# Attention in two passes, with the row maxima carried through DRAM into a 97th row of the queries

## The reference

```python
scale = 1.0 / math.sqrt(QK_NOPE + QK_ROPE)          # 1 / sqrt(96)
s = einsum('bqhd,bkhd->bhqk', qn_b, k_nope) + einsum('bqhd,bkd->bhqk', qr_b, k_rope)
p = jax.nn.softmax(s.astype(jnp.float32) * scale, axis=-1)
return jnp.einsum('bhqk,bkhd->bqhd', p.astype(v.dtype), v)   # v: 64 columns per head
```

## Time and profile before

| | |
|---|---|
| median of three runs | 3265.0 us (3261.01 to 3273.98) |
| the profiled execution | 3276.46 us |
| its span | 3274.6 us |
| attention's first to last product | 527 to 1215 us |
| granted TensorE clock, mean of the span | 0.982 |

### The profile page before, as it was taken

The page is one execution under the profiler, slowest core; times in us unless marked ns, Lnnn a source line. Parts: engine busy times, 40 slices in busy tenths (PEclk is TensorE's granted clock), DMA queues, the critical chain, the costliest instruction groups (busy, mean ns, idle before and its releaser), DMA issues.

```text
span 3274.6 us, 54823 instructions
## 1 busy us (share of the span) xinstructions
PE 3152.3 (96%) x23414; PEld 2544.0 (78%) x23414; DVE 2012.7 (61%) x3047; ACT 1067.3 (33%) x1528; POOL 374.1 (11%) x354
## 2 busy tenths in 40 slices
PE   8998998899999998999999999999999999999999
PEld 7787886777777777778888888887746888788887
DVE  6665554466766775545444444469979988755544
ACT  5222334445444443222111111132253333433332
POOL 0222441000000000301000000020000000110000
PEclk9999999799999999999999999999999999999999
DMA  3343665122222223421111111111101222223222
GB/s 148 126 135 99 214 213 186 54 75 81 69 86 75 82 81 116 148 90 52 39 52 52 52 42 49 52 39 52 39 13 52 103 91 103 90 90 126 94 91 76
DMA packets 93537, 288.80 MB, mean 88 GB/s; under 512 B 12400, under 2 KB 38640, under 8 KB 72816
## 3 DMA queue, kind: packets, MB, share of 16 engines
q1 hardware_dynamic: 79104, 233.39, 21.1%
q0 software_dynamic: 14192, 51.91, 4.6%
HBM read 228.64 MB, written 56.62 MB: 87 GB/s over the span
## 4 chain that ended last, share of the span: by engine, by line
PE 82%; DVE 10%; ACT 2%; issue 2%; DMA 2%; POOL 1%; SPq 1%; DVEq 0%; ACTq 0%; POOLq 0%
PE ps L2441 24%; PE ps L307 21%; PE ps L489 7%; PE ps L1744 4%; PE ps L2247 3%; PE ps L2603 2%; PE ps L1755 2%; DVE Yh L2630 2%; PE ps L1767 2%; PE ps L2063 1%; PE ps L1387 1%; PE ps L1404 1%; PE ps L1008 1%; PE ps L1398 1%; DVE wlo L287 1%
## 5 line engine op out<-in xcount | busy, mean ns | idle before, releaser
L2441 PE MATMUL ps<-Hh,whi 128*128 128x512 f32 x1600 | 497.6, 392 | 1.3 <-DVE uA L2562 0.7
L283 ACT ACTIVATE whi<-raw 128x2048 fp32r<-128x2048 f32 x139 | 265.5, 1910 | 522.2 <-PE ps L307 296.1
L287 DVE TENSOR_TENSOR wlo<-raw,whi 128x2048 fp32r<-128x2048 f32 x139 | 321.2, 2311 | 95.0 <-ACT whi L283 94.6
L2441 PEld LDWEIGHTS ps<-Hh,whi 128*128 128x128 f32 x1600 | 300.0, 188 | 70.5 <-issue 5.3
L2441 PE MATMUL ps<-Hh,wlo 128*128 128x512 f32 x800 | 311.4, 389 | 0.0
L307 PE MATMUL ps<-Hhi,wlo 128*128 128x512 f32 x672 | 206.9, 389 | 0.0
L307 PE MATMUL ps<-Hlo,whi 128*128 128x512 f32 x672 | 206.9, 389 | 0.0
L307 PE MATMUL ps<-Hhi,whi 128*128 128x512 f32 x672 | 206.8, 389 | 0.0
L2441 PE MATMUL ps<-aHh,whi 128*128 128x512 f32 x512 | 199.5, 390 | 2.7 <-DVE wlo L287 2.5
L2441 PE MATMUL ps<-aLh,whi 128*128 128x512 f32 x512 | 199.2, 389 | 0.0
L2441 PE MATMUL ps<-aHh,wlo 128*128 128x512 f32 x512 | 199.2, 389 | 0.0
(11 more groups left out here) (389 smaller groups left out, 6181.8 us busy)
## 6 DMA issues: line engine op xcount, KB each, us to landing
raw<-in_panels SPq DMA_DIRECT2D x139, 1024.0 KB, 4.8
rwf<-F POOLq DMA_DIRECT2D x16, 1280.0 KB, 6.6
L<-rwf SPq DMA_DIRECT2D x16, 1024.0 KB, 5.0
L<-rwf SPq DMA_DIRECT2D x64, 256.0 KB, 3.5
gts<-so POOLq DMA_DIRECT2D x16, 512.0 KB, 3.5
gl<-gts SPq DMA_DIRECT2D x32, 256.0 KB, 3.6
rwt<-so POOLq DMA_DIRECT2D x15, 512.0 KB, 2.9
qkd<-XTs POOLq DMA_DIRECT2D x16, 384.0 KB, 4.0
```

What stands on the lines that cost most here:

```text
L283: e.activation(whi[i % 2][:, :], raw_of(i)[:, :], AF.Copy).then_inc(*a_hi.up(i))
L287: e.tensor_tensor(wlo[i % 2][:, :], raw_of(i)[:, :], whi[i % 2][:, :].bitcast(F32), OP.subtract).then_inc(*v_lo.up(i))
L2441: m = e.matmul(ap, W[wi][:, kc, n0:n0 + 128], mov[mi][:, kc, :], start=x == 0 and q == 0, stop=x == len(kcs) - 1 and q == 2)
```

## The change

The attention goes by eight groups g (a pair of heads k = g // 2 and a half of the queries), and each group has two passes of eight items:
- "max" j: scores of one head and 128 queries as before, but from tiles typed fp32r, into banks 4 and 5; VectorE takes the negated maxima into negm.
- the row: when a group's eight maxima are there, GpSimd's queue stores the 128x8 values to DRAM as [8, 128] (nrow) and, when that has landed, loads them into the 97th partition of the queries' tile Qr. The 97th row of the keys' tile Kr is ones, written once.
- "exp" j: the scores again, transposed: 128 keys by 512 queries for both heads, in fp32 and with 97 rows, so that the maximum is subtracted by the product. ScalarE takes the exponential straight into Pe. There are no transposes and no scaling.
- PV: two products of 512 columns, accumulated over j in bank 6 or 7. The sums over keys: GpSimd adds the Pe tiles (acc), and at a group's end TensorE multiplies acc with ones (bank 4), ScalarE copies, VectorE takes the reciprocal of 128x512, multiplies, and GpSimd stores.
The maxima pass of group g + 1 alternates with the exponent pass of group g. `slots()` stays as it was; the items are laid over its pieces.

```diff
-    Kp = [sb(f"Kp{i}", 8 * i, [96, 2, S]) for i in range(2)]
...
+    Kr = [sb(f"Kr{i}", 8 * i, [97, 2, S], F32R) for i in range(2)]
+    Pe = [sb(f"Pe{i}", 16 + 4 * i, [128, 2, 512]) for i in range(2)]
+    acc = sb("acc", 24, [128, 2, 512])
+    Qr = [sb(f"Qr{i}", (28, 170, 174)[i], [97, 2, 512], F32R) for i in range(3)]
...
+    def att_items():
+        made = [("max", 0, j) for j in range(8)]
+        for g in range(7):
+            made += [("max", g + 1, 0)]
+            for j in range(7):
+                made += [("max", g + 1, j + 1), ("exp", g, j)]
+            made += [("exp", g, 7)]
+        return made + [("exp", 7, j) for j in range(8)]
...
+            if c == "exp":
+                on.setdefault(i + (2 if g < 7 else 1), []).append(("PV", g, j))
+                on.setdefault(i + 1, []).append(("acc", g, j))
+                if j == 7:
+                    on.setdefault(i + (4 if g < 6 else 3 if g < 7 else 2), []).append(("sum", g, 0))
+                    on.setdefault(i + (5 if g < 6 else 4 if g < 7 else 3), []).append(("out", g, 0))
+            if c == "max" and j == 7:
+                on.setdefault(i + (2 if g else 1), []).append(("row", g, 0))
...
     def att_pe(e, u, c):
...
+            if name == "sum":
+                pair_free(e, "sum", g, 0)
+                e.wait_ge(*g_at.by("acc", g, 7))
+                for h in range(2):
+                    m = e.matmul(bank[4][64 * h:64 * h + 64, :], ones[:, 0:64], acc[:, h, :], start=True, stop=True)
...
+            if name == "max":
...
+                pair_free(e, "max", g, j)
+                for half in range(2):
+                    m = e.matmul(bank[4 + half], Qr[g % 3][0:96, j % 2, 128 * (j // 2):128 * (j // 2) + 128],
+                                 Kr[k % 2][0:96, j % 2, hs(half)], start=True, stop=True)
...
+                if j == 0:
+                    e.wait_ge(*d_nr.by(g, "in"))
...
+                for h in range(2):
+                    m = e.matmul(bank[4 + h], Kr[k % 2][:, h, 128 * j:128 * (j + 1)].bitcast(F32),
+                                 Qr[g % 3][:, h, :].bitcast(F32), start=True, stop=True)
...
+                e.wait_ge(*a_at.by("E", g, j))
+                for h in range(2):
+                    m = e.matmul(bank[6 + g % 2][64 * h:64 * h + 64, :], Vp[(g // 2) % 2][:, j, 64 * h:64 * h + 64],
+                                 Pe[j % 2][:, h, :], start=j == 0, stop=j == 7)
...
     def att_dve(e, u, c):
...
+        if i == 0:
+            for n in range(2):
+                e.memset(Kr[n][96:97, :, :].bitcast(F32), 1.0).then_inc(*v_at.up("ones", n))
...
+                e.reciprocal(Oh[:, :], Oh[:, :]).then_inc(*v_at.up("rec", g))
...
+                e.tensor_tensor(Oh[:, :], bank[6 + g % 2], Oh[:, :], OP.mult).then_inc(*v_at.up("O", g))
...
     def att_pool(e, u, c):
...
+            if name == "row":
+                e.wait_ge(*v_at.by("max", g, 7))
+                e.dma_start(nrow[g].rearrange("n q -> q n"), negm[:, 8 * g:8 * g + 8], allow_slow_non_contiguous=True).then_inc(*d_nr.up(g, "out"))
+                e.wait_ge(*d_nr.by(g, "out"))
+                if g >= 3:
+                    e.wait_ge(*t_at.by("B", g - 3, 7))
+                e.dma_start(Qr[g % 3][96:97, :, :].bitcast(F32), nrow[g].rearrange("(h n) q -> h (n q)", h=2)[None, :, :]).then_inc(*d_nr.up(g, "in"))
+            if name == "acc" and j:
...
+                e.tensor_tensor(acc[:, :, :], Pe[0][:, :, :] if j == 1 else acc[:, :, :], Pe[j % 2][:, :, :],
+                                OP.add).then_inc(*g_at.up("acc", g, j))
...
-        for k in range(2):
+        for k in range(3):
             q_sp(e, k)
```

More of the change, by code:

```diff
@@ L1713, in build @@
[L1713 to L1716, removed]
-    oas = dram("oas", [4, 128, S])
-    t_at, v_at, a_at = signals("t_at"), signals("v_at"), signals("a_at")
-    d_kp, d_vp, d_qb, d_oa = landings("d_kp", 2), landings("d_vp", 2), landings("d_qb", 3), landings("d_oa", 2)
+    negm = sb("negm", 40, [128, 64])
+    Oh = sb("Oh", 201.28125, [128, 512])
@@ new lines, in build @@
+    oas = dram("oas", [4, 128, S])
+    nrow = dram("nrow", [8, 8, 128])
+    d_nr = landings("d_nr", 2)
+    t_at, v_at, a_at, g_at = signals("t_at"), signals("v_at"), signals("a_at"), signals("g_at")
+    d_kp, d_vp, d_qr, d_oa = landings("d_kp", 2), landings("d_vp", 2), landings("d_qr", 3), landings("d_oa", 1)
+    def att_items():
[6 more added lines that the diff above has]
+        return made + [("exp", 7, j) for j in range(8)]
@@ new lines, in build, with also @@
+    ITEMS = att_items()
+    def also():
+        on = {}
+        for i, (c, g, j) in enumerate(ITEMS):
+            if c == "exp":
[6 more added lines that the diff above has]
+                on.setdefault(i + (2 if g else 1), []).append(("row", g, 0))
+        return on
@@ L1721, in kv_sp, with before_of @@
+    ALSO = also()
+    def before_of():
+        made, last = {}, None
+        for i in range(len(ITEMS) + 4):
+            for key in [key for key in ALSO.get(i, ()) if key[0] == "sum"] + ITEMS[i:i + 1]:
+                made[key], last = last, key
+        return made
+    PAIR = before_of()
     def kv_sp(e, k):
         if k >= 2:
-            e.wait_ge(*t_at.by("S", 16 * k - 17))
-            e.wait_ge(*t_at.by("O", 8 * k - 9))
-        e.dma_start(Kp[k % 2][:, :, :], qkd[1, :, 2 * k:2 * k + 2, :]).then_inc(*d_kp.up(k))
+            e.wait_ge(*t_at.by("B", 2 * k - 3, 7))
+            e.wait_ge(*t_at.by("PV", 2 * k - 3, 7))
+        e.dma_start(Kr[k % 2][0:96, :, :].bitcast(F32), qkd[1, :, 2 * k:2 * k + 2, :]).then_inc(*d_kp.up(k))
@@ L1726, in kv_sp @@
         e.dma_start(Vp[k % 2][:, :, :], vds[:, :, 128 * k:128 * (k + 1)]).then_inc(*d_vp.up(k))
     def q_sp(e, g):
-        k, j = g // 8, g % 8
+        k, qh = g // 2, g % 2
         if g >= 3:
-            e.wait_ge(*t_at.by("S", 2 * g - 5))
-        e.dma_start(Qb[g % 3][:, :, :], qkd[0, :, 2 * k:2 * k + 2, 128 * j:128 * (j + 1)]).then_inc(*d_qb.up(g))
-    def att_pe(e, u, c):
[L1735 to L1768, removed]
@@ new lines, in att_act @@
+    def att_act(e, u, c):
+        i = 2 * u + c
+        for name, g, j in ALSO.get(i, ()):
+            if name == "sum":
+                e.wait_ge(*t_at.by("sum", g))
+                if g:
+                    e.wait_ge(*d_oa.by(g - 1))
+                e.activation(Oh[:, :], bank[4], AF.Copy).then_inc(*a_at.up("sum", g))
+        if i < len(ITEMS):
+            name, g, j = ITEMS[i]
+            if name == "exp":
+                e.wait_ge(*t_at.by("B", g, j))
+                n = 8 * g + j - 2
+                if n >= 0:
+                    e.wait_ge(*t_at.by("PV", n // 8, n % 8))
+                    e.wait_ge(*g_at.by("acc", n // 8, max(1, n % 8)))
+                e.activation(Pe[j % 2][:, :, :], ps[:, 2048:3072].rearrange("p (h t) -> p h t", h=2),
+                             AF.Exp).then_inc(*a_at.up("E", g, j))
@@ L1822, in build @@
+    def att_sp(e, u, c):
+        i = 2 * u + c - 8
+        if i >= 0 and i % 16 == 5:
+            g = i // 16 + 2
+            if 3 <= g < 8:
+                q_sp(e, g)
+            if g in (4, 6):
+                kv_sp(e, g // 2)
     BEFORE = ("cum", "mul", "turn", "scores", "PV", "Nc")
@@ L1932, in att_over @@
         e.wait_ge(*a_at.all())
+        e.wait_ge(*g_at.all())
+        for w in d_nr.all():
+            e.wait_ge(*w)
         for w in d_oa.all():
```

96 lines of the change are left out of this document (49 added, 47 removed).

## The result

The changed kernel takes 3403.8 us (median of four, 3380.5 to 3416.8) against 3268.5 us of the kernel before, run beside it: ratio 1.041, 95% interval 1.034 to 1.047. That is 135 us slower, where 10 us of the profiled execution's time were forecast and the range ended at 3315. The forecast was wrong. The profiled execution is the one of 3380.5 us, so what follows shows about 104 of the 135 us.

The account below looks back on a forecast made before the run. TensorE, busy 96% of the span, was taken as the bound. Terms -25 - 10 + 25 + 15 + 1 + 4 = +10 us gave 3286.5 for the profiled execution, 3275 in terms of the median; range 3237 to 3315.

Parts of the forecast that it names:

- TensorE's work, -25: Attention matmuls: maxima, exponent, PV and sum products take 226 us against 251 with transposes, 25 us less.
- ScalarE, -10: TensorE's 16.1 us of waits for ScalarE's copies: the transposes' 6.9 go, part of L1358's 9.2 stays, 10 us less.
- "out", +25: Group ends: VectorE's reciprocal and multiply, 4.04 us in one piece, delay TensorE 3.3 us each; 25 us more for eight.
- GpSimd's additions, +15: 56 additions of Pe tiles hold up VectorE's instructions with two SBUF operands, 0 to 60 us; 15 us more taken.
- its worst case: Rival: VectorE and GpSimd hold each other for most of each addition, +45 us, 3310; chance 0.18.
- The row, +5 in all: Row of maxima through DRAM: trip of 9.4 us, free in six groups, 1 us more in the last, 4 in the first.
- The rival of the late row: Row's trip decides from 15 us on; at 22 us it costs 63 more, +73, 3338; chance 0.08.
- The clock: Rival: new gaps bring four more stretches of 10 us at 1.2 GHz, 5 us each, +20, 3295; chance 0.10.

Follow-up runs that it names:

- e1: Changed kernel without the row's store and load, the 97th row of Qr set once at the start: 3338.1 us, ratio 1.022.
- e4: Changed kernel without the row's trip, without reciprocals and with 8 of the 56 additions: 3309.2 us, ratio 1.013.
- h2: e4 without ScalarE's copy of bank 4, sum products kept, VectorE copying the PV bank in place of the multiply: 3278.6 us, ratio 1.003.
- f4: e4 without sum products and ScalarE's copy of bank 4, VectorE copying the PV bank in place of the multiply: 3272.3 us, ratio 1.001.
- e2: Changed kernel without the eight reciprocals of 128x512, PV multiplied with the sums as they are: 3378.2 us, ratio 1.034.
- h1: f1 with the reciprocal in four pieces of 128 columns and the memsets of Kr's 97th row on GpSimd: 3330.3 us, ratio 1.019.
- e3: Changed kernel with 8 of the 56 additions on GpSimd, one for each group: 3382.3 us, ratio 1.037.
- f1: Changed kernel with the row made by a TensorE transpose, a ScalarE copy and one DMA from SBUF: 3329.9 us, ratio 1.019.
- f2: Changed kernel with the row's store in 128 pieces of 32 B instead of 1,024 of 4 B: 3322.5 us, ratio 1.016.
- g2: f2 with the store made four times, each after the landing of the one before: 3340.0 us, ratio 1.022.

## Why the forecast failed, step by step

From the changed kernel down: 3403.8, less 66 (trip, e1), less 29 (reciprocals and additions behind it, e4), less 31 (the copy of the sum, h2), less 6 (the sum's products, f4) is 3272. Two steps of the prediction failed with effect: the price of the row's store, and ScalarE's eight copies taken as an exchange.

- **TensorE's work, -25.** Right in kind, too large. At the higher clock a maxima pair is 0.62 to 0.73 us in the chain, not 0.55: 64 times some 0.15 is 10 us. A PV pair is 1.01, not 0.95: 4 us. That makes it -11; without the sums -19, and f4 shows 16.6 less busy time, at a clock of 0.94 for 0.95.
- **ScalarE, -10.** L1358's wait fell from 9.2 to 1.6 and the transposes' went, as said. But "it gains eight copies of the sums where it had eight of Oh" was taken for an exchange. The old copy held a bank that nobody needed soon; the new one holds bank 4, which the next product needs. This step failed: 31 us, in none of the terms and none of the rivals.
- **"out", +25.** Measured 26 with the trip in place (e2, within its noise). Its reason was half right: the wait for RG grew by 7 us, but by h1 it is VectorE's load that counts there, not the place of the 3.35 us.
- **GpSimd's additions, +15.** Measured 21 (e3), inside the bounds but not clear of noise. Two-operand instructions did get longer, as said: L1570 went from 683 to 871 ns and L1555 from 686 to 849, and in e3, with 8 of the 56 additions, they are back at 685 and 684; L1550 stayed at 686. L1660 is another case. It went from 690 to 975, but in e3 it is at 1039, since it falls together with a group's first addition, which e3 and e4 keep. One such pair in e3:
```profile
690.91 2.33 POOL L1870 TENSOR_TENSOR acc<-Pe,Pe 128x1024 f32<-128x1024 f32 x1
...
691.27 2.53 DVE L1660 TENSOR_TENSOR Os<-Os,sc 128x512 f32<-128x512 f32 x1
```
  The addition ends at 693.24, the VectorE instruction 0.56 us later: it stood until the addition was over. So the mechanism of the prediction is right, its worst case does occur, and e3's 21 us leave a part of it out. Together these reciprocals and additions are 29 us without the trip.
- **The row, +5 in all.** The step that failed with the largest effect: some 66 to 81 us (e1, f1, f2) for 5. The prediction had the store at 6 us, "nearest to rwf" in number of pieces; it took 10.2, the trip 18 in place of 9.4. The rival of the late row, with a chance of 0.08, foresaw such a trip (22 us, 63 more), but its mechanism was right only for the first and last group (10.7 and 6.2 us, where it had 13 each): it was to decide from 15 us on, and the six groups between, with 7 us each, hid 18. That its 63 lies near the 66 measured is luck. What was in no term is that the store holds up other transfers: loads of 3 to 6 us took 15, and TensorE stood still for nothing shown. The prediction weighed the rule of the Trainium skill (DMA: Bandwidth & Descriptors, "Rules for kernel authors") as bearing on the trip's length alone. By f2 the rule, one descriptor per element and to be arranged otherwise, was worth 81 us.
- **The clock.** Four more stretches of 10 us at the lower level were given 0.10. In the steady part alone there are 110 us more at the lower level, worth 55 by the prediction's own price. We read it as no cause of its own: with the parts taken out it went from 0.89 to 0.93 (e4), 0.97 (h2) and 0.98 (f4), and parts gave back more than their waits.

The chances followed from the terms: TensorE has no room, so every mistake in what holds it back was a mistake on one side.

## What to carry to other kernels

Cost a transfer not only by who waits for it but by its number of pieces and by what else moves meanwhile; here 4 KB in pieces of one element held up loads of 256 KB and 1 MB. When a new consumer of a bank takes an old one's place, name the next writer of that bank: a copy of 0.59 us cost some 4 us each time here. In a kernel bound by TensorE, price a new gap at its length and the time at the lower clock behind it.

## What the runs showed that was not expected

- 1,024 pieces of 4 B landed in 10.2 us, the same 4 KB as 128 pieces of 32 B in 2.8. While one of the first kind ran (937.5 to 946 us), all DMA together moved 0 to 109 GB/s.
- A load of one row of 4 KB into one partition took 6.3 us in the changed kernel, and 1.9 (g2) and 4.0 (f2) where no small pieces were written.
- A memset of 2,048 elements on one partition took 1.76 us (forecast 2.2).
- Making the row by a transpose, a copy of 0.25 us and a DMA of eight pieces of 512 B (3.8 us to landing) cost no more than leaving it out (3329.9 against 3338.1).
